# RWKV scan: the squares of the chunk inverse go to TensorE's two other quadrants, and the wanted rows' products are spread between the records of levels 2 and 3

## The reference, cut to what matters

```
def step(S, inp):
    r_t, w_t, k_t, v_t, kk_t, a_t = inp
    sa = jnp.einsum('bhvk,bhk->bhv', S, -kk_t)
    S = (S * w_t[:, :, None, :] + sa[..., None] * (kk_t * a_t)[:, :, None, :]
         + v_t[..., None] * k_t[:, :, None, :])
    return S, jnp.einsum('bhvk,bhk->bhv', S, r_t)
```

## Time and profile before

| what | value |
|---|---|
| median of three executions | 2648.25 us |
| the profiled execution | 2646.26 us |
| its span | 2644.5 us |
| the scan's 16 chunks, from the first X0 to the last read-out | about 434 to 856 us |
| an even and an odd chunk together, in the middle | 52.3 us |

### The profile page before, as it was taken

The page is one execution under the profiler, slowest core; times in us unless marked ns, Lnnn a source line. Parts: engine busy times, 40 slices in busy tenths (PEclk is TensorE's granted clock), DMA queues, the critical chain, the costliest instruction groups (busy, mean ns, idle before and its releaser), DMA issues. The chain is left out here.

```text
span 2644.5 us, 42291 instructions
## 1 busy us (share of the span) xinstructions
PE 2529.2 (96%) x17850; PEld 1351.2 (51%) x17850; DVE 980.2 (37%) x1819; ACT 579.5 (22%) x996; POOL 407.7 (15%) x423
## 2 busy tenths in 40 slices
PE   5999998999999997999999989999899799999998
PEld 3344445998998553443344344444855443334443
DVE  7335434667675344111111134224844611111114
ACT  4443001344444221000000011311643100000000
POOL 0022420223332101000000002211011100100000
PEclk8999999999999998999999999999999899999999
DMA  3334334332231617999999861252461689999997
GB/s 127 145 134 145 118 112 160 87 90 79 67 102 33 263 64 268 388 427 421 416 426 427 372 247 72 88 182 79 146 208 56 246 325 425 425 419 426 427 428 290
DMA packets 216552, 618.83 MB, mean 234 GB/s; under 512 B 40193, under 2 KB 157058, under 8 KB 189746
## 3 DMA queue, kind: packets, MB, share of 16 engines
q1 hardware_dynamic: 188946, 534.69, 52.7%
q10 hardware_dynamic: 14288, 48.25, 4.6%
q0 software_dynamic: 13136, 33.25, 3.2%
HBM read 540.96 MB, written 89.66 MB: 238 GB/s over the span
## 5 line engine op out<-in xcount | busy, mean ns | idle before, releaser
L2550 PE MATMUL moe_psum<-trunk_late,moe_x_t 128*64 128x512 f32 (+2 forms) x912 | 344.2, 593 | 0.9 <-DVE moe_x_t L2677 0.9
L2509 DVE TENSOR_TENSOR moe_buffers_both<-moe_buffers_both,moe_psum 128x512 f32<-128x512 f32 x46 | 49.9, 1084 | 625.2 <-ACT moe_buffers_both L2723 625.2
L2550 PE MATMUL moe_psum<-trunk_early,moe_x_t 128*64 128x512 f32 (+2 forms) x512 | 216.3, 604 | 2.5 <-ACT moe_x_t L2021 2.5
L2550 PEld LDWEIGHTS moe_psum<-trunk_late,moe_x_t 128*64 128x64 f32 (+2 forms) x912 | 121.4, 151 | 162.3 <-issue 161.2
L2550 PE MATMUL moe_psum<-trunk_mixed,moe_x_t 128*64 128x512 f32 (+2 forms) x448 | 181.9, 593 | 0.0
L2565 POOL DMA_INDIRECT expert_rows<-moe_buffers_out,moe_scatter_row x45 | 45.9, 1020 | 868.9 <-DVE moe_buffers_out L2689 860.7
L1863 PE MATMUL moe_psum<-trunk_late,trunk_mixed 128*128 128x512 f32 x384 | 169.2, 594 | 0.0
L2723 ACT ACTIVATE moe_buffers_both<-moe_psum 128x512 f32<-128x512 f32 x46 | 27.5, 597 | 613.2 <-PE moe_psum L2550 613.2
L2550 PE MATMUL moe_psum<-trunk_kept,moe_x_t 128*128 128x512 f32 (+2 forms) x368 | 147.9, 593 | 0.9 <-DVE moe_x_t L2677 0.9
L1450 PE MATMUL scan_psum<-scan_xp,scan_x 64*64 64x128 f32 (+1 forms) x2560 | 140.0, 250 | 4.3 <-issue 3.6
L2550 PE MATMUL moe_psum<-trunk_late,moe_buffers_act_t 128*64 128x512 f32 (+2 forms) x304 | 134.2, 594 | 0.0
(11 more groups left out here) (519 smaller groups left out, 4376.5 us busy)
## 6 DMA issues: line engine op xcount, KB each, us to landing
trunk_late<-in_moe_w_in SPq DMA_DIRECT2D x49, 2048.0 KB, 19.9
trunk_early<-in_moe_w_in SPq DMA_DIRECT2D x28, 2048.0 KB, 20.9
trunk_mixed<-in_moe_w_in SPq DMA_DIRECT2D x22, 2048.0 KB, 22.4
trunk_kept<-in_moe_w_in SPq DMA_DIRECT2D x19, 2048.0 KB, 23.7
trunk_mixed<-in_moe_w_out SPq DMA_DIRECT2D x18, 2048.0 KB, 24.4
trunk_early<-in_moe_w_out SPq DMA_DIRECT2D x18, 2048.0 KB, 25.4
trunk_late<-in_moe_w_out SPq DMA_DIRECT2D x15, 2048.0 KB, 22.1
trunk_ninth<-in_moe_w_out SPq DMA_DIRECT2D x10, 2048.0 KB, 22.7
```

Source lines behind the costliest of these rows:

```text
L2509: return v.tensor_mul(self.act[:].rearrange("p (k q) -> p k q", k=FF // P), self.silu[:].rearrange(by_row, k=FF // P), self.value_p.rearra ...
L2550: mm = t.matmul(psum[rows, bank + a, :], left[:, k0 + k, rows], weights.units[unit.slot][:, k, a * HALF:(a + 1) * HALF], start=(part != "h ...
```

## The change

The squares of levels 0 to 4 are written to the partitions `own[head]`, so they take the two quadrants that the factor products leave free (`other[head]` to `own[head]`). Squares and factor products of a pair alternate in the program, and a half's level starts when all its three inputs are there (X, X' and P; in level 0 the masked KB and the copied rows), where the squares before did not wait for P. X comes out on the wrong half of the partitions, so ScalarE copies it by two activations of 64 partitions each, which cross over, in place of one of 128. W.0 is issued in pieces in level 2, W.1 in level 3; a piece is 2 matmuls and follows a pair's squares and factor product. The pieces use the quadrants of the squares. ScalarE copies W.0 after X4 and W.1 after X5, and the doubled keys come after W.1's copy.

```diff
+        WANTED_LEVELS = (2, 3)
...
-                            a.activation(x[j % 2][:, half[h], :], slim(X_BANK + h), ACT.Copy).then_inc(act.sem, 1)
+                            for head in range(2):
+                                back = a.activation(x[j % 2][other[head], half[h], :], slim(X_BANK + h)[own[head]], ACT.Copy)
+                            back.then_inc(act.sem, 1)
+                        if j == LEVELS - 1:
+                            keep_wanted(0, chunk)
...
-                    for h in range(2):
-                        a.wait_ge(pe.sem, pe.after(f"W.{h}", chunk))
-                        a.activation(w_st[:, half[h], :], slim(kb_bank(h)), ACT.Copy, scale=-1.0).then_inc(act.sem, 1)
-                        if h == 0 and (b == 0 or not last):
-                            twice(chunk + 1, 1 - b)
+                    keep_wanted(1, chunk)
+                    if b == 0 or not last:
+                        twice(chunk + 1, 1 - b)
...
+            def squares(h, x_old, xp_old, columns, between=None):
+
+                for m in range(half[h].start, half[h].stop):
+                    at = m - half[h].start
+                    for head in range(2):
+                        square = t.matmul(slim(X_BANK + h)[own[head], at, :], xp_old[other[head], m, 0, :],
+                                          x_old[other[head], m, :], start=True, stop=True)
+                    if m == half[h].stop - 1:
+                        square.then_inc(pe.sem, 1)
+                    for head in range(2):
+                        factor = t.matmul(wide(XP_BANK + h)[other[head], at, columns], x_old[other[head], m, :],
+                                          xp_old[other[head], m].rearrange("p a t -> p (a t)")[:, columns],
+                                          start=True, stop=True)
+                    if m == half[h].stop - 1:
+                        factor.then_inc(pe.sem, 1)
+                    if between is not None:
+                        last = between(PAIRS // 2 * h + at)
+                return last if between is not None else None
...
                             t.wait_ge(act.sem, act.after(f"X{j}.{h}", chunk))
+                            t.wait_ge(dve.sem, dve.after(f"P{j - 1}.{h}", chunk))
                             t.wait_ge(dve.sem, dve.after(f"XT{j}.{h}", chunk))
-                            each_head(slim(X_BANK + h), half[h], xt, x[old])
-                            t.wait_ge(dve.sem, dve.after(f"P{j - 1}.{h}", chunk))
-                            if j < LEVELS - 1:
-                                each_head(wide(XP_BANK + h), half[h], x[old],
-                                          xp[old][:].rearrange("p m a t -> p m (a t)"))
-                            else:
-                                each_head(wide(XP_BANK + h)[:, :, CHUNK:P], half[h], x[old], pt)
+                            if j not in WANTED_LEVELS:
+                                squares(h, x[old], xp[old], slice(0, P) if j < LEVELS - 1 else slice(CHUNK, P))
+                                continue
+                            if j == WANTED_LEVELS[0] and h == 0:
+                                t.wait_ge(dve.sem, dve.after("S.1", chunk - 1))
+                                t.wait_ge(mask.sem, mask.after("R.1", chunk))
+                                t.wait_ge(v_in[b], 32 * trip + 32)
+                                if chunk == 0:
+                                    t.wait_ge(ready, 1)
+                            mm = squares(h, x[old], xp[old], slice(0, P), wanted(WANTED_LEVELS.index(j), b, a_b))
+                            if h == 1:
+                                mm.then_inc(pe.sem, 1)
```

54 lines of the change are left out of this document (29 added, 25 removed).

## The result

The changed kernel took 2656.79 us at the median of 12 runs (2652.9 to 2661.26), the kernel before 2647.87 us beside it. The ratio is 1.0035, with an interval of 1.0028 to 1.0043. It is slower, by 9 us, where the forecast was 35 us faster. The profiled execution took 2655.7 us.

What follows compares the result with a forecast made beforehand. PE was taken to bound each chunk, VectorE next. Eight odd chunks (13.7 us), seven even ones (19.1) and chunk 0 (2) give 35 us together: 2611 for a run like the profiled one, 2613 at the median, range 2603 to 2634.

Steps and rivals of the forecast that it cites:

- The quadrants' pace: On PE, four independent quadrants: 58 ns a record (64 columns), 109 ns (128); halves of levels 2 and 3 take 0.93 us.
- the second case: Rival: PE's records come no closer than 24.8 ns over long stretches, so only 15 us are won: 2633; chance 0.16.
- the third: Rival: squares and factor products on PE don't overlap, so the kernel is 14 us slower: 2662; chance 0.06.
- the last sentence of the sum: VectorE's delays are what is left; PE's longest new gap, 0.8 us before U, is shorter than gaps seen at full clock.
- the fourth case: Rival: the gain is lost elsewhere, by a clock dropping in new gaps or a late transfer: about 2646; chance 0.05.
- Won: 2.73 us: Walk through the even chunk: U of half 1 starts at 614.14 and not 616.87, 2.73 us won.
- Won: 1.71 us: Walk through the odd chunk: U of half 0 starts at 641.19 and not 642.90, 1.71 us won.
- L1288 (1.49) until 640.80: Odd chunk before U: VectorE's decayed keys take 1.49 us after P4 ends at 639.40, then first P5 at 641.13.
- I take 0.66: ScalarE's two crossed copies for a half: 0.66 us, the second starting 0.28 after the first; bounds 0.38 and 1.08.
- The level's turn: Levels 1 to 3: a turn of 1.90 us, bound by PE and VectorE together, where it was 2.68.
- "Issue" as a cost: In chunk 0 PE stands still, part of 11.5 us of "issue"; 0 to 3 us won there, 2 taken.
- the forecast's first case: Four quadrants on PE overlap as walked through: 2613, own range 2604 to 2624; chance 0.73.

Runs made afterwards that it cites:

- run 4: The changed kernel plus filling products nobody reads, 2 at the head of level 0 in each chunk, 3 before U in odd chunks: 2642.77 us.
- run 9: The changed kernel with late keys (next chunk's decayed keys behind U's copies) and tile loads of one pair in eight from the second trip: 2628.16 us.
- run 13: The changed kernel with late keys, tile loads of one pair in eight from the second trip, and X copied whole by one instruction: 2616.7 us.
- run 5: The changed kernel with late keys: the next chunk's decayed keys behind U's copies on VectorE, doubled keys behind ScalarE's copies of U: 2632.28 us.
- run 1: The changed kernel with each tile load bringing one pair of eight (64 KB, not 512 KB) from the second trip on: 2658.11 us.
- Run 12: The changed kernel with late keys and two filling products at the head of level 0 in each chunk: 2632.20 us.
- run 8: The changed kernel with late keys, loads of kk and r moved to the even chunk, v and gate behind the odd chunk's last product: 2634.41 us.

## Why the prediction was wrong

**What held.** The quadrants' pace was right, in all its sizes: a half of levels 2 and 3 takes 0.93 us with W in it, one of levels 0 and 4 0.47, and the records come 1.86 us / 96 = 19 ns apart over 96 records, below the 24.8 ns of the second case. That case and the third are out. The even chunk's level 4 waits for ScalarE's copies and U for the last sum behind the keys, as forecast.

**The steps that failed** are two. One is the last sentence of the sum: "VectorE's delays are what is left: the longest new gap on PE is 0.8 us before U, shorter than what the timeline shows at full clock", and with it "nothing in the rows asks for it" in the fourth case, which had 0.05. The mechanism named there, a clock that drops in the new gaps, is what happened. The gap before U was 1.2 us in the odd chunk, PE had been busy for only 4.70 of 8.60 us up to there, and then the read-out ran at 1.2 GHz. I had compared one gap with one gap. What had changed was how much PE stood still in the whole stretch: the change lets its products overlap and gives the other engines more to do. The clock is 14 of the 44 us between forecast and result; without it the change would be at 2643 (run 4), still outside the range.

The other is the two walks that the sum is made of, "Won: 2.73 us" and "Won: 1.71 us". At full clock an even chunk takes 23.67 us against 25.39 before: 1.72 won, 1.0 short. An odd one takes 26.89 against 26.6, the mean of the six that can be timed before from the second trip on: 0.3 lost, 2.0 short. In seven and eight chunks that is 7 and 16 us. Chunk 0 took 1.2 us longer, where 2 were to be won. With the clock's 14 this makes 40 of the 44. The terms below are where these walks were off.

Hiding the keys gives back 24.5: some 14 by the clock, and 1.4 us in each odd chunk (25.50 against 26.89, in the trips where no stop costs anything).

**The terms that were mis-sized:**
- The keys, "L1288 (1.49) until 640.80": 2.13 us measured in the odd chunk, 2.71 with squares alone, 3.23 with small loads. Alone the two take 1.29. The 1.49 was already a key that met the tail of a GpSimd product (0.89 and 0.68 us). The change brings VectorE to the keys sooner behind ScalarE's exponential and so deeper under GpSimd's products, and there a key ends 0.55 us behind the product, however early it began. The walk had the keys wait for VectorE's queue alone; in the odd chunk GpSimd and the exponential ahead of it set their end.
- The crossed copies, "I take 0.66": 0.78 a pair, back to back. ScalarE's busy time in the scan rose by 61.6 us (179.2 to 240.8), not 45. The step that the second would start 0.1 before the first's end was wrong, and the order of work made it matter at one place more: the odd chunk's XP5 waits for the second exponential and a pair of copies, and my walk through the odd chunk had its wait only for VectorE. In the odd chunks from the second trip on, the gap from PE's last start to that of XP5 is 1.1 to 1.7 us in run 9, and 0.3 to 1.1 with whole copies (run 13).
- The level's turn. From level 2 to 3 it is 2.22 us in both chunks. The walk had 2.03 in the even chunk and 2.23 in the odd one, behind VectorE's running sum, so the odd one is as forecast. From level 3 to 4 the walk had 2.10 and 1.91; measured are 2.53 (616.25 to 618.78) and 2.34 (747.83 to 750.17). Late keys alone leave them (2.23 and 2.53 from 654.84, run 5); with whole copies (run 13, from 688.16 and 711.61) they are 2.00 and 2.01 in the even chunk, 2.23 and 2.01 in the odd one. So but for the running sum it was the crossing, behind the logarithms, the root and the exponential on ScalarE.
- "Issue" as a cost: I read it only in chunk 0. As soon as PE ran through its records faster, the instruction fetch behind a 512 KB load came too late in odd chunks as well.

**The account.** From 2657 us: hiding the keys takes off 24.5, with the clock's 14 in it as far as run 4 tells. What then stands between 2632 and 2617 is the fetch and the crossing, 15.6 us together in run 13. That 2617 lies in the range of the forecast's first case, 2604 to 2624, is no proof of its sum: the sum had bare keys and crossed copies in it, and run 13 has neither. What is confirmed is the pace of the quadrants.

**Open.** Which part of the waits makes the clock fall. In run 5 PE stopped for 1.44 and 1.57 us and stayed at full clock with 6.36 busy of 10.5 us; in run 1 it fell behind a wait of 1.45 us without any stop; in the changed kernel's chunk from 734.46 it didn't fall at all. Run 12's fill in one place changed nothing. Also open is how much of the keys' cost is their being bare and how much GpSimd's products: late keys take away both.

## What to carry to other kernels

When a change shortens the products of the bounding engine, list every instruction on the other engines that lay under them, and cost it bare, at the place where it will then stand. Moving it is part of the change: here that alone turned 9 us slower into 16 us faster. Look at what else runs at that place too: here GpSimd's products set the end of the keys. And run the two parts of a change apart: the squares alone were 9 us faster from the first. Ask then what each part still carries of the other, as the pieces alone, 29 us slower, carried the joint wait.

Where two supplies are near their limit together (here ScalarE's copies and the instruction fetch), relieving one shows next to nothing: 4 and 5 us alone, 16 together, more clearly in the traces than in the medians.

## What the runs showed of the hardware

- All four quadrants of TensorE run at once. Float32 products of 64 and of 128 columns keep 58 and 109 ns a record in each quadrant at full clock while the others run, and starts in different quadrants lie 19 ns apart on average over 96 records.
- PE's instructions came in packets of 16 KB for 252 records. With 512 KB loads on the way PE stood still for up to 2.8 us (run 8), in the changed kernel each time at record 3 to 6 of a block of 252, and 1.2 to 1.6 us behind the landing of a packet. With loads of 64 KB these stops were gone (run 1) or at most 1.1 us long (runs 9 and 13).
- Work that leaves TensorE less busy can slow it: 34 us at half clock in the changed kernel, 65 with the stops taken away, none in the kernel before in the same stretch. In the chunks where the clock fell, no single wait of PE ahead of the fall was as long as 2 us.
- VectorE's product of two 128x512 tiles takes 0.68 us alone. Begun under a GpSimd product of that kind, it ended 0.55 us behind the end of GpSimd's, 63 times of 63, and took up to 1.72 us.
- ScalarE's copies of 64 partitions take 0.38 us, the same as those of 128, and a pair starts 0.39 to 0.41 us apart; so splitting by partition doubles the time.
